# Prompt attention of a hybrid decoder step: query heads paired on array halves, keys in one-bank pieces with a running maximum, the probabilities scaled on GpSimd, the loop over head pairs written out

## The reference, cut to what matters

```python
def _masked_softmax(logits, mask):
    p = jax.nn.softmax(jnp.where(mask, logits, NEG), axis=-1)
    return jnp.where(mask, p, 0.0)
...
    logits = jnp.einsum('bnqgrd,bnsgd->bngrqs', qb, kb).astype(jnp.float32) * SM_SCALE + bias.astype(jnp.float32)
...
    o = jnp.einsum('bngrqs,bnsgd->bnqgrd', p.astype(v.dtype), vb)
```

## Time and profile before

| | |
|---|---|
| median of 3 runs | 1246.25 us (1245.88 to 1246.71) |
| the profiled execution, span | 1247.6 us |
| TensorE busy (matmul records) | 1113.3 us, 89% |
| VectorE busy | 726.0 us, 58% |
| ScalarE busy | 394.5 us, 32% |
| GpSimd busy | 57.9 us, 5% |
| mean granted TensorE clock | 0.959 of full |

### The profile page before, as it was taken

How to read it: one execution, slowest core, us unless ns; L and a number is a source line. 1 busy time by engine, 2 the same in 40 slices (tenths; PEclk the granted TensorE clock), 3 DMA queues, 4 the chain that set the end, 5 groups by cost and what they waited for, 6 DMA issues and landing times.

```text
span 1247.6 us, 15439 instructions
## 1 busy us (share of the span) xinstructions
PE 1113.3 (89%) x5232; PEld 692.1 (55%) x5232; DVE 726.0 (58%) x1249; ACT 394.5 (32%) x835; POOL 57.9 (5%) x55
## 2 busy tenths in 40 slices
PE   2997999984949999987999999999999888889997
PEld 2564664542525667655666666666665555554442
DVE  3157999998987996136656666666663223321121
ACT  3110201222211101226446446446445445321010
POOL 0001110000011000000000000000001010000000
PEclk9998999987879997998999999999999999999999
DMA  9145553001245221306000000000004746441111
GB/s 294 55 79 207 202 179 123 25 9 34 84 152 178 93 93 43 129 38 226 1 2 0 0 0 0 0 0 0 0 0 185 288 165 281 184 178 68 67 59 42
DMA packets 26325, 117.37 MB, mean 94 GB/s; under 512 B 2553, under 2 KB 10891, under 8 KB 19659
## 3 DMA queue, kind: packets, MB, share of 16 engines
q0 software_dynamic: 7056, 68.16, 14.7%
q1 hardware_dynamic: 17925, 44.95, 10.8%
q10 hardware_dynamic: 1311, 3.83, 1.1%
HBM read 107.95 MB, written 13.29 MB: 97 GB/s over the span
## 4 chain that ended last, share of the span: by engine, by line
PE 55%; DVE 20%; issue 6%; DVEq 5%; DMA 5%; PEld 5%; ACT 3%; ACTq 0%; PEldq 0%; SPq 0%
PE PS L1630 10%; PE PS L757 10%; PE PS L1319 9%; PE PS L1344 9%; DVE main L601 7%; DVE half L567 6%; PE PS L1329 5%; DMA main<-in_cmp_k_dram,row 3%; PE PS L1518 3%; PE PS L1510 3%; DMA main<-in_x_prompt_dram 2%; DVE main L565 2%; DVEq L566 2%; PE PS L721 2%; PEld PS L1562 2%
## 5 line engine op out<-in xcount | busy, mean ns | idle before, releaser
L757 PE MATMUL PS<-main 128*128 128x352 f32 (+1 forms) x1152 | 361.8, 477 | 27.7 <-ACTq L397 18.8
L757 PEld LDWEIGHTS PS<-main 128*128 128x128 f32 x1152 | 222.5, 194 | 164.2 <-ACTq L397 19.3
L1344 PE MATMUL PS<-main 128*64 128x128 f32 x1056 | 152.6, 279 | 0.5
L1319 PE MATMUL PS<-main 128*128 128x512 f32 (+3 forms) x388 | 134.6, 481 | 9.1 <-ACT main L1240 3.7
L1235 ACT ACTIVATE main<-PS 128x512 f32<-128x512 f32 (+3 forms) x192 | 89.1, 464 | 169.0 <-PE PS L1329 166.9
L1344 PEld LDWEIGHTS PS<-main 128*64 128x64 f32 x1056 | 113.9, 137 | 20.8 <-issue 15.9
L1630 PE MATMUL PS<-main 128*128 128x512 f32 (+1 forms) x288 | 124.0, 593 | 0.8 <-DVEq L1492 0.8
L567 DVE TENSOR_REDUCE half<-main 128x128 f32<-128x2048 f32 x32 | 117.0, 3656 | 2.4
L1319 PEld LDWEIGHTS PS<-main 128*128 128x128 f32 x388 | 66.1, 192 | 66.8 <-issue 53.3
L394 ACT ACTIVATE main<-PS 128x384 f32 (+1 forms) x24 | 11.8, 492 | 281.9 <-PE PS L757 281.3
L1329 PE MATMUL PS<-cst,main 128*128 128x128 f32 x528 | 95.8, 286 | 4.8 <-ACT main L1235 2.0
(11 more groups left out here) (286 smaller groups left out, 989.7 us busy)
## 6 DMA issues: line engine op xcount, KB each, us to landing
main<-in_w_tiles_dram SPq DMA_DIRECT2D x24, 512.0 KB, 3.5
main<-in_x_prompt_dram SPq DMA_DIRECT2D x16, 512.0 KB, 4.9
out_dram<-main SPq DMA_DIRECT2D x12, 512.0 KB, 2.6
main<-in_w_out_dram SPq DMA_DIRECT2D x1, 4096.0 KB, 12.0
diag<-in_win_k_dram SPq DMA_DIRECT2D x8, 256.0 KB, 11.7
diag<-in_win_v_dram SPq DMA_DIRECT2D x8, 256.0 KB, 11.2
out_dram<-in_win_k_dram SPq DMA_DIRECT2D x1, 2016.0 KB
out_dram<-in_win_v_dram SPq DMA_DIRECT2D x1, 2016.0 KB
```

The lines of the kernel that those rows point to most:

```text
L757: last = pe.matmul(bank(3 * s + j)[:, 0:n], ring[:, s, k * P:(k + 1) * P], xT[:, k, t0:t0 + n], start=(k == 0), stop=(k == KD - 1))
L1319: last = pe.matmul(bank(2 * br, 2)[:, a:a + m], qpad[:, g, i * P:(i + 1) * P], proj[:, (KS, KW)[br], k0 + a:k0 + a + m], start=True, stop= ...
L1344: last = pe.matmul(o, nat[:, br, t, g * HD:(g + 1) * HD], pt[:, c % 2, e * P:(e + 1) * P], start=False, stop=end)
```

## The change

- **Head pairs.** A group is now (r, i) with both g. The scores of the two heads are two matmuls over 64 rows each, on rows 0 to 63 and 64 to 127 of the array, straight from `proj`; `qpad` and `queries` go. The values of the two heads alternate, on columns 0 to 63 and 64 to 127. Odd r go through the tiles backwards.
- **Pieces.** The keys of a branch are cut into the last 4 tiles and the (up to 4) before them, so that a piece of one head fits one bank; four banks hold two steps. Bias, mask and maximum are one Vector instruction in place. A branch with two pieces keeps a maximum and a sum for each, and joins them afterwards: a subtraction, a small exponential on ScalarE, two fused operations, a reciprocal and a product.
- **Scaling** moves from VectorE to GpSimd (`pool_pairs`), which stands in GpSimd's queue between the first gather of cached keys and the wait for the cached values' room.
- **Turned probabilities** of up to 4 units (2 tiles x 2 heads in each bank) are copied half by ScalarE, half by VectorE, into `pt`, which moves to `late`.
- **Order.** One list of 98 slots, written out without a loop: a slot has one step (a piece of both heads) and, when the scaled probabilities are due, one cycle (transposes of up to 4 units; their values come in the next slot). There are 96 steps and 76 cycles.
- `psel` and `pwin` have three buffers. The third lies in `nat`, where the natural keys and compressed-branch rows are, so ScalarE waits for all of `nat_out` before the first exponential.

```diff
+        GROUPS = [(r, i if r % 2 == 0 else NT - 1 - i) for r in range(R) for i in range(NT)]
...
+        def chunks_of(i, br):
+            ts = tiles_of(i, br)
+            return [ts[-4:]] if len(ts) <= 4 else [ts[:-4], ts[-4:]]
...
+        SLOTS, nc_ = [], 0
+        while len(SLOTS) < NS or nc_ < NCY:
+            n = len(SLOTS)
+            ready = nc_ < NCY and n >= last_step[CYCLES[nc_][0], CYCLES[nc_][1][-1][0]] + 2
+            SLOTS.append((n if n < NS else None, nc_ if ready else None))
+            nc_ += ready
...
-            dve.memset(qpad[HD:P, 0, :], 0.0)
-            dve.memset(qpad[0:HD, 1, :], 0.0)
-            for g in range(G):
-                rows = slice(g * HD, (g + 1) * HD)
-                dve.tensor_copy(qpad[rows, g, :], proj[rows, QT, 0:T])
...
         def act_pairs(act):
             act.wait_ge(SEM["vb_ready"], 1)
+            act.wait_ge(SEM["nat_out"], 16 * N_NAT)
+            for s, c in SLOTS:
...
+                    for g in range(G):
+                        act.wait_ge(SEM["mx"], G * s + g + 1)
+                        act.activation(p_tile(k, br)[:, g, off:off + n], bank(2 * (s % 2) + g)[:, 0:n], ACT.Exp,
+                                       bias=st(k, MB if whole else MA, br, g), scale=1.0 if plain else -1.0,
+                                       accum_out=st(k, LB if whole else LA, br, g)).then_inc(SEM["ex"], 1)
+                    if whole and (k, br) in split:
+                        act.wait_ge(SEM["apart"], split.index((k, br)) + 1)
+                        act.activation(st(k, CA, br), st(k, DA, br), ACT.Exp).then_inc(SEM["corr"], 1)
+                if c is not None:
...
+                    act.activation(pt[:, 0, 0:n], bank(4)[:, 0:n], ACT.Copy).then_inc(SEM["pt_sb0"], 1)
...
+                            dve.tensor_tensor_reduce(b, b, table, -1.0, -NEG if nch == 1 and n != 3 * P else st(k, MA, br, g),
+                                                     ALU.add, ALU.min, st(k, MB, br, g)).then_inc(SEM["mx"], 1)
...
+                        for g in range(G):
+                            dve.scalar_tensor_tensor(st(k, LA, br, g), st(k, LA, br, g), st(k, CA, br, g), st(k, LB, br, g), ALU.mult, ALU.add)
+                        dve.drain()
+                        dve.reciprocal(st(k, W_, br), st(k, LA, br))
+                        dve.drain()
+                        dve.tensor_tensor(st(k, WA, br), st(k, W_, br), st(k, CA, br), ALU.mult).then_inc(SEM["w_ready"], 1)
...
+                    dve.wait_ge(SEM["pt_ps1"], n_second[c])
+                    dve.tensor_copy(pt[:, 1, 0:n], bank(5)[:, 0:n]).then_inc(SEM["pt_sb1"], 1)
...
+        def pool_pairs(pool):
+            n = 0
+            for k, (r, i) in enumerate(GROUPS):
+                for br in range(2):
+                    n += 1
+                    pool.wait_ge(SEM["w_ready"], n)
+                    for a, ts in enumerate(chunks_of(i, br)):
...
+                        for g in range(G):
+                            p = p_tile(k, br)[:, g, off:off + len(ts) * P]
...
+                            pool.tensor_scalar(p, p, st(k, W_ if whole else WA, br, g), gate, ALU.mult, ALU.mult).then_inc(SEM["p_ready"], 1)
...
+                for e, (br, t) in enumerate(units):
+                    for g in range(G):
+                        a = (e % 2 * G + g) * P
+                        last = pe.matmul(o[g], nat[:, br, t, g * HD:(g + 1) * HD], pt[:, e // 2, a:a + P],
+                                         start=False, stop=end and e + 1 == len(units))
...
+                    if s >= 2:
+                        pe.wait_ge(SEM["ex"], G * (s - 1))
+                    for g in range(G):
+                        rows = slice(g * HD, (g + 1) * HD)
+                        last = pe.matmul(bank(2 * (s % 2) + g)[:, 0:len(ts) * P], proj[rows, QT + r, i * P:(i + 1) * P],
+                                         proj[rows, (KS, KW)[br], ts[0] * P:(ts[-1] + 1) * P], start=True, stop=True)
+                    last.then_inc(SEM["qk"], 1)
+                if n_slot and SLOTS[n_slot - 1][1] is not None:
+                    values(SLOTS[n_slot - 1][1])
```

More of the change, by code:

```diff
@@ L884, in program @@
         osb = kcn_flat[:, 768:896]
+        pt = late[:, 0:2 * 512].rearrange("p (b n) -> p b n", b=2)
+        stat = sb("stat", [P, 3, 8, 2 * G])
         gd = sb("gd", [P, 4, 3])
@@ new lines, in program @@
+        NCY = len(CYCLES)
+        n_second = [sum(len(c[1]) > 2 for c in CYCLES[:n + 1]) for n in range(NCY)]
+        last_cycle = {c[0]: n for n, c in enumerate(CYCLES)}
+        SLOTS, nc_ = [], 0
[4 more added lines that the diff above has]
+            nc_ += ready
+        slot_of = {c: n for n, (s, c) in enumerate(SLOTS) if c is not None}
@@ L1194, in dve_pairs_prepare, with st, p_tile @@
+        for k in range(3, NG):
+            assert slot_of[last_cycle[k - 3]] <= first_step[k] + 1
+        SLOTS += [(None, None)] * 2
+        MA, MB, LA, LB, CA, W_, WA, DA = range(8)
+        def st(k, what, br, g=None):
+            a = br * G + (g or 0)
+            return stat[:, k % 3, what, a:a + (G if g is None else 1)]
+        def p_tile(k, br):
+            return (psel, pwin)[br][k % 3]
         def dve_pairs_prepare(dve):
@@ L1216, in following @@
-        def following(k, r):
-            return (k, r) if k < NU else (0, r + 1)
         def act_pairs(act):
-            for _ in range(2):
-                act.drain().then_inc(SEM["pt_sb"], 1)
             act.wait_ge(SEM["vb_ready"], 1)
[L1224 to L1248, removed]
-                    evac(k - 1, 0, r)
-                    exp(k1, 0, r1)
-                    evac(k - 1, 1, r)
-                    exp(k1, 1, r1)
-                    if k < NU and UNITS[k][1] == 1:
-                        queries(UNITS[k][0], r + 1)
@@ L1348, in pe_pairs @@
-            for br in range(2):
-                scores(0, br, 0, first=True)
-            with pe.Fori(0, R) as r:
-                late_chunk = None
-                for k in range(1, NU + 1):
-                    k1, r1 = following(k, r)
-                    chunks = [(c, k - 1, br, ts) for br in range(2) for c, ts in chunk_of[k - 1, br]]
-                    for br in range(2):
-                        scores(k1, br, r1)
-                    for chunk in chunks:
-                        turn(r, *chunk)
-                        if late_chunk:
-                            values(r, *late_chunk)
-                        late_chunk = chunk
-                values(r, *late_chunk)
-                pe.drain().then_inc(SEM["pair_done"], 1)
+            pe.wait_ge(strip_in, 16)
@@ new lines, in values @@
+            def values(c):
+                k, units, first, end = CYCLES[c]
+                r, i = GROUPS[k]
+                o = [bank(6 + k % 2)[g * HD:(g + 1) * HD, 0:P] for g in range(G)]
+                if first:
+                    if k >= 2:
+                        pe.wait_ge(SEM["oz"], k - 1)
+                    for g in range(G):
+                        pe.matmul(o[g], vb[:, r, g * HD:(g + 1) * HD], ptc[:, i, g, :], start=True, stop=False)
+                pe.wait_ge(SEM["pt_sb0"], c + 1)
+                pe.wait_ge(SEM["pt_sb1"], n_second[c])
+                for e, (br, t) in enumerate(units):
+                    for g in range(G):
+                        a = (e % 2 * G + g) * P
+                        last = pe.matmul(o[g], nat[:, br, t, g * HD:(g + 1) * HD], pt[:, e // 2, a:a + P],
+                                         start=False, stop=end and e + 1 == len(units))
+                if end:
+                    last.then_inc(SEM["o_ps"], 1)
```

222 lines of the change are left out of this document (109 added, 113 removed).

## The result

| | before | after |
|---|---|---|
| median | 1246.07 us (4 runs, 1238.94 to 1246.71) | 1150.48 us (4 runs, 1145.73 to 1159.06) |
| ratio | | 0.9239, 95% interval 0.9186 to 0.9291 |
| profiled execution, span | 1247.6 us | 1157.2 us |

A second timing of the same kernel, with the last experiments, gave 1151.37 us (6 runs, ratio 0.9248, 0.9209 to 0.9287). Medians of one kernel differ by up to 7 us from set to set (the kernel before: 1241.15 to 1248.07), so experiments are compared by the stage in their traces as well: from the first exponential to the samples' first transposes. I call that "the stage". A second trace of the changed kernel gave 271.4 us where the first gave 274.9, so differences under 4 us say nothing.

What follows compares the result with a forecast made beforehand. TensorE was taken to bound the kernel. Slots from 582.7 us, plus 252, 19, 2 and 2.3, end at 858, a gain of 88.8 us from 1247.6: 1158 us forecast, own range 1137 to 1183, wider range 1133 to 1203.

Steps and rivals of the forecast that it cites:

- Row halves run together: Scores of two heads on TensorE: they overlap wholly, 56.3 us instead of 112.7.
- rival 1: Scores on TensorE: row halves don't overlap, 56.3 us more on TensorE, about 42 showing, 1200 us in all; chance 0.1.
- Column halves: Values matmuls on TensorE: alternating halves does twice the work in the same time, 16 records in 1.03 us.
- TensorE's sum of 218 us: TensorE's work in the stage: values 63.3, transposes 56.5, scores 56.3 us, plus switches 12.9, 12.9 and 16.3.
- the lower level only at the start: TensorE's clock after some 15 us without matmuls: lower in the small first slots, costing 2 us.
- VectorE's sum of 226 us: VectorE's work in the stage: 101 us for 192 instructions, 50 for joins, 40 for copies and smaller items; 240 before.
- lead in 42 slots: Slot-by-slot count over 98 slots: VectorE is the largest term in 42, TensorE in 24, the two-slot loop in 32.
- GpSimd at 0.9 us for 512 columns, 4 us of lateness: Scaling of probabilities on GpSimd: 0.9 us per 512 columns, some 130 us in all; late pieces add 4 us.
- Rival 2: GpSimd's scaling delivers late: at 1.5 us a piece, about 35 us more, 1193 us in all; chance 0.14.
- The stage, 276 us from 582 to 858: First exponential to the samples' part: slots 252 us, unevenness and late GpSimd pieces 19, clock 2, tail 2.3.
- The loop over two slots: Scores, maxima, second exponential, ScalarE's copy, values, next transposes: half of this chain sets the length of 32 slots.
- The start, 582: First exponential at about 582: transfers end at 584.3, everything comes 3.0 us earlier without `qpad`, then 0.5 us.

## Why the prediction was right, step by step

**Row halves run together** (rival 1, 0.1): shown, 1.06 us a pair against 1.92 on one half. By its own price the prediction would have been 42 us off without it. The experiment gives 51 us of the stage, 37 with the clock taken out and 55 by the ratio, so the price can stand.

**Column halves**: as the earlier trace rows had it, 1.03 us for 16 records.

**TensorE's sum of 218 us**: the matmul records were busy for 228 to 248 us in the kernels whose matmuls were left as they are. Part of the surplus goes with the clock: at 705.23 one group took 1.90 us. The prediction had the lower level only at the start, at 2 us; there it lasted 9.6 us, 4.4 by the estimate of 0.46. The clock dropped again inside the stage, which the prediction had named as what would make it wrong, without a price. These later drops cost some 6 us in the first trace and 3 in the second, by the same estimate; no run changed the clock alone.

**VectorE's sum of 226 us**: mis-sized. It was busy for 179.3. VectorE's timeline of the changed kernel:

```profile
640.73 0.35 DVE L1303 SCALAR_TENSOR_TENSOR stat<-stat 128x1 f32<-128x1 f32 x2 [0.16 <-issue]
641.15 0.17 DVE L1305 RECIPROCAL stat<-stat 128x2 f32<-128x2 f32 x1
641.39 0.16 DVE L1307 TENSOR_TENSOR stat<-stat 128x2 f32<-128x2 f32 x1
641.58 0.76 DVE L1286 CUSTOM_DVE_ANT_0 PS<-PS,diag,stat 128x512 f32<-128x512 f32 x1
642.26 0.14 DVE L1286 DVE_READ_ACCUMULATOR2_ANT stat<- 128x1 f32 x1
642.26 0.76 DVE L1286 CUSTOM_DVE_ANT_1 PS<-PS,diag,stat 128x512 f32<-128x512 f32 x1
```

The accumulator's read (0.14 us) begins together with the next instruction, so a 512-column piece costs 642.26 - 641.58 = 0.68 us with it, where 0.69 + 0.08 had been put. The join takes from 640.73 to 641.55 us, 0.8 us, where 1.2 had been put. That VectorE did not lead in 42 slots is inferred from its busy time (65% of the stage) and from the experiment, in which scaling on it cost 25 us, not 35 to 60.

**GpSimd at 0.9 us for 512 columns, 4 us of lateness**: the duration was nearly right (0.771), the lateness was the term that was mis-sized. Three slots instead of two took 20 to 23 us off the stage, some 17 with the clock taken out; the 36 us less work on GpSimd alone took 4. The prediction had compared two pieces (2 x 0.9) with the 2.1 us left in a full slot; after a thin slot the slot is shorter, and GpSimd's floor of 0.34 us, the four pieces of a thick branch and the join stand in one line. Rival 2, late delivery, was real at half to two thirds of its price (35 us) and was part of the outcome, not another outcome.

By the Trainium skill ("GPSIMD Engine Reference", section 3.1) 512 columns take 769 ns at best, which is its 1.8 cycles an element. The trace agrees at this width only, with 771: at 128 columns the same 1.8 cycles would give 192 ns (an estimate from the page's figure), and 449 were measured. The table in section 4.1 of the same page of the Trainium skill, which names VectorE and not GpSimd for elementwise work, is right for the duration (VectorE 541 ns in the experiment) and not for this stage: VectorE's version was 25 us slower, 17 with the clock taken out.

**The stage, 276 us from 582 to 858**: measured 274.9 and 271.4. The agreement is partly luck: VectorE's overestimate (47 us of busy time) and the underestimated lateness and clock offset each other. The loop over two slots was there, but the copy's place was worth only some 5 us.

**The start, 582**: 585.3 in the trace, and 578.0 to 584.1 in eight other traces with the same start, so 582 lies inside the scatter. In this trace the outputs' wait was 16.16 us and uncovered, as said, but the transfers ended at 583.98, 0.3 us earlier than before and not 3.0; and the 0.5 us from there to the first exponential left out the table load of 1.28 us. Order and a later wait win back 12 us in the ratio.

**The rest**: the samples' part took 297.0 us against 300.8; nothing of the change is in it, and it varies from 294.3 to 300.6 us in the other traces. The profiled span, 1157.2 us, is 1.6 below the 1158.8 of the forecast: 2.2 more up to the samples' part, 3.8 less in it. Most of the 7.5 us comes of it that the profiled execution was the slowest of the four (1159.06 against a median of 1150.48). The forecast's last step is also a slip: 1158.8 less 1.35 is 1157.5, not 1158.

## What to carry to other kernels

When a probability or any other tile passes over four engines, count the line from the last producer to the first consumer, with joins and floors, and give it one slot more than the sums of full slots say; then check how many buffers that slot needs, for here one slot too few cost 18 to 23 us and one too many 12. Put the new wait that a reused buffer brings at the first use of that buffer, and order the work so that the thick pieces stand before it. Matmuls on two column halves pay in full only when neighbours alternate; for row halves no other order was tried. And before a difference between two traces is put down to an edit, compare how long the clock was at its lower level in each.

## What the runs showed of the hardware that had not been expected

- Four values matmuls on one column half followed by four on the other take 1.46 us for 16 records; alternating, 1.03. Why the first is not 1.7 and more stays open.
- A Vector instruction of 512 columns with an accumulator (757 ns) and the next of its kind start 0.68 us apart, with the read (142 ns) between them, so that the read costs the engine next to nothing.
- TensorE's clock fell to 1.2 GHz for some 3 us at a time inside a stage in which TensorE was 88% busy (0.50 granted at 681 to 683 us), where the kernel before, 97% busy, kept 1.00 behind its start. The number of drops differed between two traces of the same kernel, four and two, and with them the stage by 3.5 us.
- With the scores on one row half the clock stayed at 1.2 GHz for 43 us at the stage's start, although the matmul records left no gap in most of it; in one execution, and why stays open. Busy time by stretch in that kernel:

```profile
588.00:618.00 30.00, 30.00 (x114) 17.86 (x114) 11.09 (x42) 10.44 (x33) 6.73 (x10) 0.50 0.00 1
```

- A GpSimd scaling of 128 columns costs 449 ns, of 512 columns 771.
